# Last output projection: seven block products in place of eight for units 2 to 7

## What is computed

```python
y = jnp.concatenate([y_sb, y_lru], axis=-1)
h = h + jnp.einsum('bse,ed->bsd', y, w_out[l])
```

## Time and profile before

| | before |
|---|---|
| median of three runs | 2098.05 us (2097.89 to 2100.16) |
| profiled execution, span | 2098.9 us |
| PE, DVE, ACT, POOL busy | 99%, 68%, 47%, 9% of the span |
| unit 1 of the last projection ends, units 2 to 7 start | 1964.8 us |
| last matmul starts | 2095.29 us |

### The profile page before, as it was taken

One profiled execution on the slowest core, in us unless ns is written; L12 is line 12 of the kernel. 1 busy time (PEld: TensorE's weight loads), 2 busy tenths in 40 slices (PEclk: granted clock), 3 DMA queues, 4 the chain that ended last, 5 costly groups with the idle time before them and its releaser, 6 DMA issues. The chain is left out here.

```text
span 2098.9 us, 30066 instructions
## 1 busy us (share of the span) xinstructions
PE 2082.9 (99%) x9702; PEld 1734.5 (83%) x9702; DVE 1417.7 (68%) x2581; ACT 996.4 (47%) x1928; POOL 191.2 (9%) x197
## 2 busy tenths in 40 slices
PE   9999999999999999999999999999999999999999
PEld 7888888888888888888888788888888888888887
DVE  6677777777733568888888633677777677868432
ACT  6444444445422446666666633544454545446221
POOL 0111111112101000000000122200000000003000
PEclk9999999999999999999999999999999999999999
DMA  7324444445733624444444734533434334345742
GB/s 227 100 72 113 111 112 114 113 114 170 210 83 97 196 63 122 126 127 127 127 127 118 250 95 115 170 106 86 121 101 133 87 108 119 109 114 156 218 112 70
DMA packets 409917, 264.40 MB, mean 126 GB/s; under 512 B 20480, under 2 KB 382720, under 8 KB 409856
## 3 DMA queue, kind: packets, MB, share of 16 engines
q1 hardware_dynamic: 401120, 255.87, 43.1%
q10 hardware_dynamic: 8736, 7.74, 1.5%
HBM read 210.33 MB, written 24.12 MB: 112 GB/s over the span
## 5 line engine op out<-in xcount | busy, mean ns | idle before, releaser
L639 PE MATMUL pp<-act_hi,w_hi 128*128 128x512 f32 x2304 | 903.1, 392 | 6.9 <-DVE w_lo L613 4.2
L641 PE MATMUL pp<-act_hi,w_lo 128*128 128x512 f32 x2304 | 898.2, 390 | 0.0
L640 PE MATMUL pp<-act_lo,w_hi 128*128 128x512 f32 x2304 | 897.9, 390 | 0.0
L613 DVE TENSOR_TENSOR w_lo<-raw,w_hi 128x512 fp32r<-128x512 f32 x680 | 457.1, 704 | 360.7 <-ACT w_hi L605 359.8
L605 ACT ACTIVATE w_hi<-raw 128x512 fp32r<-128x512 f32 (+1 forms) x684 | 396.2, 622 | 456.2 <-PE pp L641 231.3
L639 PEld LDWEIGHTS pp<-act_hi,w_hi 128*128 128x128 f32 x2304 | 433.1, 188 | 100.9 <-DVE w_lo L613 6.0
L641 PEld LDWEIGHTS pp<-act_hi,w_lo 128*128 128x128 f32 x2304 | 432.9, 188 | 91.1
L640 PEld LDWEIGHTS pp<-act_lo,w_hi 128*128 128x128 f32 x2304 | 433.2, 188 | 87.3 <-issue 0.2
L658 POOL TENSOR_TENSOR pT_lo<-gathered,pT_hi 128x640 fp32r<-128x640 f32 x30 | 46.5, 1571 | 358.9 <-ACT pT_hi L654 358.9
L1318 ACT ACTIVATE prob<-ps,minus,q_scale 128x512 f32<-128x512 f32 (+1 forms) x64 | 39.0, 615 | 78.3 <-DVE minus L1398 78.3
L639 PE MATMUL ps<-act_hi,w_hi 128*128 128x512 f32 x176 | 69.3, 394 | 0.0
(11 more groups left out here) (435 smaller groups left out, 2755.1 us busy)
## 6 DMA issues: line engine op xcount, KB each, us to landing
raw<-w_in SPq DMA_DIRECT2D x48, 1024.0 KB, 5.9
raw<-swa_w_in SPq DMA_DIRECT2D x36, 1024.0 KB, 5.8
raw<-mla_w_in SPq DMA_DIRECT2D x23, 1024.0 KB, 5.7
raw<-mla_w_out SPq DMA_DIRECT2D x16, 1024.0 KB, 6.5
raw<-swa_w_out SPq DMA_DIRECT2D x16, 1024.0 KB, 6.1
raw<-w_out SPq DMA_DIRECT2D x16, 1024.0 KB, 6.9
gathered<-turned SPq DMA_DIRECT2D x224, 56.0 KB, 2.0
x_feature_major<-xT SPq DMA_DIRECT2D x8, 1024.0 KB, 9.7
```

The costliest lines, as they stand in the source:

```text
L613: q.eng.tensor_tensor(dst, raw_piece(tile, p), high, ALU.subtract).then_inc(s_lo, tile.ups(p))
L639: q.eng.matmul(psum[:, :], wh, ah, start=start and n == 0, stop=False)
L640: q.eng.matmul(psum[:, :], wh, al, start=False, stop=False)
L641: last = q.eng.matmul(psum[:, :], wl, ah, start=False, stop=stop and n == PIECE // P - 1)
```

## The change

Units 2 to 7 no longer take 16 chunks by 512 tokens in one sum. Each unit is a 2 by 2 block product: two output tiles (rows), two halves of the 16 chunks (inner), two halves of the tokens (`early`, `late`, 256 each). Seven products of 8 chunks by 256 tokens replace the eight: `11`, `12`, `22` on plain blocks, `s1`, `s2`, `s3` on sums of y blocks, and `s4` with a sum of weight blocks; `s1` to `s4` all use sums of weight blocks. A product is 24 matmuls of 128 by 256, in a PSUM bank of its own. Units 0 and 1 are made as before.

- `y_sums_G`: five steps on GpSimd, behind its last `act_lo`, make the y sums: (1) `chain` = late minus early of chunks 0 to 7; (2) chunk 15 put together again; (3) `chain` = late of chunks 8 to 15 minus `chain`; (4) late of 8 to 15 minus late of 0 to 7; (5) early of 8 to 15 minus `chain`. Steps 1, 3, 4 and 5 have 2048 elements in each partition. Chunks 8 to 14 are loaded again from HBM into `xT`, 1.75 MB, by a transfer that SP starts behind L844 and L845. `y_sums_A` and `y_sums_V` make the high and low halves of the four sums, 2048 elements each.
- Weights come as four blocks of 1024 columns for each unit, each with its own semaphore. `weight_sums` makes four sums of blocks on DVE, `split_hi` and `split_lo` the halves of the seven factors, in a ring of four places.
- ACT copies product `11`; DVE makes three partial sums and four final sums of 256 columns, and scales the old x; GpSimd adds partial sums to the old x, four times 256 columns for each unit.
- In the first unit of this kind DVE's order is: the four low halves of the y sums, weight sums `s1` and `s3`, old x twice, the low halves of `11` and `12`, then what is left of unit 1, then the low half of `s1` and so on.
- The two stores of a unit count on a semaphore each, and unit 1 puts its result into `acc` and `root`, since `d_y` is still read.

```diff
--- before.py
+++ after.py
+PLAIN_LAST = 2
+HALF_K, HALF_S = KC // 2, S // 2
+PRODUCTS = ("11", "12", "s1", "s2", "s3", "s4", "22")
+RING = (2, 3, 0, 1)
...
+        chain = low[:, 0:HALF_K * HALF_S].rearrange("p (c n) -> p c n", c=HALF_K)
+        w_sum = low[:, 8 * HALF_S:12 * HALF_S]
+        p1_sum, q_sum, u_sum = (low[:, (12 + n) * HALF_S:(13 + n) * HALF_S] for n in range(3))
...
+            q.eng.dma_start(xT[:, HALF_K:KC - 1, :], y_dram[HALF_K:KC - 1].rearrange("c p s -> p c s")).then_inc(s_ycopy, 16)
+            q.eng.wait_ge(s_lo, Tile("out3", PLAIN_LAST - 1, 1).count(PIECES - 1))
+            for b in ("11", "12", "22", "21"):
+                block(PLAIN_LAST, b)
+            store_out(q, 0, 0)
+            store_out(q, 0, 1)
+            q.eng.wait_ge(s_tlo, 4)
+            q.eng.dma_start(xT[:, HALF_K:KC, :], old_x(HALF_K, KC)).then_inc(s_xload[1], 16)
+            store_out(q, 1, 0)
+            store_out(q, 1, 1)
+            for i in range(PLAIN_LAST, units):
+                n = i - PLAIN_LAST
+                if i + 1 < units:
+                    q.eng.wait_ge(s_wsum, 4 * n + 3)
+                    q.eng.wait_ge(s_wlo, split_of(i, "11"))
+                    block(i + 1, "11")
+                    q.eng.wait_ge(s_wlo, split_of(i, "s3"))
+                    block(i + 1, "21")
+                    q.eng.wait_ge(s_wlo, split_of(i, "s4"))
+                    block(i + 1, "12")
+                    q.eng.wait_ge(s_wlo, split_of(i, "22"))
+                    block(i + 1, "22")
+                store_out(q, i, 0)
+                store_out(q, i, 1)
...
+        def strassen_T(q):
+            for i in range(PLAIN_LAST, KC // 2):
+                n, first = i - PLAIN_LAST, i == PLAIN_LAST
+                for product in PRODUCTS:
+                    q.eng.wait_ge(s_wlo, split_of(i, product))
+                    if product == "11":
+                        if first:
+                            q.eng.wait_ge(*q.at("V.x0", 0))
+                        else:
+                            q.eng.wait_ge(s_part, n)
+                    if first and product == "12":
+                        q.eng.wait_ge(*q.at("V.x1", 0))
+                    if product in ("12", "s4", "22") and not first:
+                        q.eng.wait_ge(s_new, 4 * (n - 1) + {"12": 1, "s4": 3, "22": 4}[product])
+                    if product in ("s2", "s1", "s3") and not first:
+                        q.eng.wait_ge(s_sums, 3 * (n - 1) + 1 + ("s2", "s1", "s3").index(product))
+                    if first and product == "22":
+                        q.eng.wait_ge(*q.at("V.x0", 1))
+                    if first and product in ("s1", "s2", "s3", "22"):
+                        q.eng.wait_ge(s_tlo, 1 + ("s1", "s2", "s3", "22").index(product))
+                    high, low_ = ring_of(i, product, w_hi), ring_of(i, product, w_lo)
+                    for c in range(HALF_K):
+                        cols = slice(c * P, (c + 1) * P)
+                        m = products(q, product_bank(product), (high[:, cols], low_[:, cols]), y_of(product, c),
+                                     c == 0, c == HALF_K - 1)
+                    m.then_inc(s_product, 1)
...
+        def y_sums_A(q):
+            places = y_sum_places()
+            late = slice(HALF_S, S)
+            q.eng.wait_ge(*q.at("V.y", phase="stick", body=H3))
+            for n, (dst, src) in enumerate(((t1[:, 0], chain), (t2[:, 0], chain), (t3[:, 0], places[1]),
+                                            (act_hi[:, 0:HALF_K, late], places[0]))):
+                q.eng.wait_ge(s_tsum, (1, 3, 3, 4)[n])
+                if n == 3:
+                    q.eng.wait_ge(s_used, Tile("out3", PLAIN_LAST - 1, 1).used(1))
+                q.eng.activation(dst, src, ACT.Copy).then_inc(s_thi, 1)
+        def y_sums_V(q):
+            places = y_sum_places()
+            late = slice(HALF_S, S)
+            for n, (dst, src, high) in enumerate(((t1[:, 1], chain, t1[:, 0]), (t2[:, 1], chain, t2[:, 0]),
+                                                  (t3[:, 1], places[1], t3[:, 0]),
+                                                  (act_lo[:, 0:HALF_K, late], places[0], act_hi[:, 0:HALF_K, late]))):
+                q.eng.wait_ge(s_thi, n + 1)
+                q.eng.tensor_tensor(dst, src, high.bitcast(F32), ALU.subtract).then_inc(s_tlo, 1)
+        def y_sums_G(q):
+            early, late = slice(0, HALF_S), slice(HALF_S, S)
+            before, after = y_sum_places()
+            last = HALF_K - 1
+            q.eng.wait_ge(*q.at("V.turned_lo", phase="stick", body=H3 - 1))
+            q.eng.wait_ge(*q.at("V.y_lru", phase="stick", body=H3 - 1))
+            q.eng.wait_ge(s_yload[0], 16 * LAYERS)
+            q.eng.tensor_tensor(chain[:, 0:last, :], y_lru[:, :, late], y_lru[:, :, early], ALU.subtract)
+            q.eng.tensor_tensor(chain[:, last, :], d_y[:, 1, late], d_y[:, 1, early], ALU.subtract).then_inc(s_tsum, 1)
+            q.eng.wait_ge(s_ylo_v, y_lo_count(KC - 1))
+            again = xT[:, KC - 1, :]
+            q.eng.tensor_tensor(again, act_hi[:, KC - 1, :].bitcast(F32), act_lo[:, KC - 1, :].bitcast(F32), ALU.add).then_inc(s_ycopy, 1)
+            q.eng.wait_ge(s_ycopy, 17)
+            q.eng.wait_ge(s_tlo, 1)
+            q.eng.tensor_tensor(chain, after, chain, ALU.subtract).then_inc(s_tsum, 1)
+            q.eng.wait_ge(s_tsum, 2)
+            q.eng.tensor_tensor(after[:, 0:last, :], after[:, 0:last, :], y_lru[:, :, late], ALU.subtract)
+            q.eng.tensor_tensor(after[:, last, :], after[:, last, :], d_y[:, 1, late], ALU.subtract).then_inc(s_tsum, 1)
+            q.eng.tensor_tensor(before, before, chain, ALU.subtract).then_inc(s_tsum, 1)
+        def split_hi(q, i, product):
+            g = split_of(i, product) - 1
+            if g < len(RING):
+                q.eng.wait_ge(s_used, Tile("out3", PLAIN_LAST - 1, 1).used(g))
+            else:
+                q.eng.wait_ge(s_product, g - len(RING) + 1)
+            n = i - PLAIN_LAST
...
+        def weight_sums(q, i, *wanted):
+            n = i - PLAIN_LAST
+            for s in wanted:
+                if s == "s1":
+                    q.eng.wait_ge(s_block["21"], 16 * (n + 1))
+                    q.eng.wait_ge(s_block["22"], 16 * (n + 1))
+                    if n:
+                        q.eng.wait_ge(s_wlo, split_of(i - 1, "s2"))
+                    m = q.eng.tensor_tensor(w_sum, raw_block("21"), raw_block("22"), ALU.add)
+                if s == "s3":
+                    q.eng.wait_ge(s_block["11"], 16 * (n + 1))
+                    q.eng.wait_ge(s_wsum, 4 * n + 1)
+                    m = q.eng.tensor_tensor(raw_block("21"), raw_block("11"), raw_block("21"), ALU.subtract)
+                if s == "s2":
+                    q.eng.wait_ge(s_wlo, split_of(i, "s1"))
+                    m = q.eng.tensor_tensor(w_sum, w_sum, raw_block("11"), ALU.subtract)
+                if s == "s4":
+                    q.eng.wait_ge(s_wlo, split_of(i, "12"))
+                    q.eng.wait_ge(s_wsum, 4 * n + 3)
+                    m = q.eng.tensor_tensor(raw_block("12"), raw_block("12"), w_sum, ALU.subtract)
+                m.then_inc(s_wsum, 1)
+        def split_lo(q, i, product):
+            q.eng.wait_ge(s_whi, split_of(i, product))
+            q.eng.tensor_tensor(ring_of(i, product, w_lo), weights_of(product), ring_of(i, product, w_hi).bitcast(F32),
+                                ALU.subtract).then_inc(s_wlo, 1)
+        def strassen_A(q):
+            for product in PRODUCTS[0:4]:
+                split_hi(q, PLAIN_LAST, product)
+            for i in range(PLAIN_LAST, KC // 2):
+                n = i - PLAIN_LAST
+                q.eng.wait_ge(s_product, split_of(i, "11"))
+                if n:
+                    q.eng.wait_ge(s_oldsum, 4 * (n - 1) + 1)
+                    q.eng.wait_ge(s_sums, 3 * (n - 1) + 1)
+                q.eng.activation(p1_sum, product_bank("11"), ACT.Copy).then_inc(s_part, 1)
+                for product in PRODUCTS[4:]:
+                    split_hi(q, i, product)
+                if i + 1 < KC // 2:
+                    for product in PRODUCTS[0:4]:
+                        split_hi(q, i + 1, product)
...
+            for i in range(PLAIN_LAST, KC // 2):
+                n, more = i - PLAIN_LAST, i + 1 < KC // 2
+                split_lo(q, i, "s3")
+                new(i, "12", 0, early, 1)
+                split_lo(q, i, "s4")
+                split_lo(q, i, "22")
+                q.eng.wait_ge(s_product, split_of(i, "s2"))
+                q.eng.wait_ge(s_part, n + 1)
+                if n:
+                    q.eng.wait_ge(s_oldsum, 4 * n)
+                q.eng.tensor_tensor(q_sum, product_bank("s2"), p1_sum, ALU.add).then_inc(s_sums, 1)
+                q.eng.wait_ge(s_sums, 3 * n + 1)
+                q.eng.tensor_tensor(u_sum, product_bank("s1"), q_sum, ALU.add).then_inc(s_sums, 1)
+                if more:
+                    scale_old(i + 1)
```

(62 more changed lines are left out.)

93 lines of the change are left out of this document (75 added, 18 removed).

## The result

The changed kernel takes 2114.78 us (median of 4 runs, 2112.44 to 2116.61); the kernel before, in the same comparison, 2099.11 (2097.89 to 2101.56). The ratio is 1.007, interval 1.0056 to 1.0084: slower by 0.7%, as forecast, and 6.9 us over the 2107.9 of the forecast. The profiled execution took 2113.65 us, of which the span is 2111.8. Above I took the span of the kernel before, 2098.9 us, for the time of its profiled execution, and that was probably 1.8 us too low. The forecast doesn't change by it: it is the median plus 9.8 us.

A forecast was written before the change was run, and what follows sets the result against it. PE alone was taken to bound units 2 to 7. The terms 2.0 + 16.0 + 2.2 - 10.0 - 0.4 = +9.8 us gave a median of 2107.9 us, with a range of 2101 to 2116.

The forecast's parts named there:

- What bounds the kernel, and the saving: Units 2 to 7: bound by PE alone; 1008 matmuls of 256 columns replace 576 of 512, saving 10.0 us.
- the 13 ns: Units 2 to 7: a matmul costs some 13 ns beside its columns, at 256 as at 512 columns.
- PE is fed in units 2 to 7: Units 2 to 7: DVE needs 17.9 to 19.9 us of PE's 20.1 in a unit; 0 taken for waits.
- Rival 3: Units 2 to 7: DVE becomes the bound, a unit takes 22 us, the kernel 2119; chance 0.06.
- The stall: Between unit 1 and first product `11`: PE waits 16.0 us behind the y sums, bounds 13.5 to 19.5.
- The last head: Last head, ahead of unit 1's end: GpSimd's step 1 slows its DVE chain, +2.0 us, bounds 0.5 to 3.0.
- The factor of 1.72: Last head: its DVE chain took 8.8 us under GpSimd's work against 5.13 with GpSimd idle.
- The low clock: Behind the stall: PE restarts at the low clock, a loss of 2.2 us, bounds 1.4 and 3.1.
- The tail: End of the kernel: a last addition of 256 columns and an earlier last matmul end give -0.4 us.
- all high bounds: Whole kernel: 2098.05 + 3.0 + 19.5 + 3.1 - 10.4 = 2113.3 us.
- Rival 1: Start of unit 2: the y sums are there in time, so faster; 2089.7 us with no stall; chance 0.09.
- rival 2: Start of unit 2: the terms cancel with a stall of 4 to 8 us, time about 2098; chance 0.08.

The follow-up runs named there:

- the halves experiment: The kernel before, with each matmul of units 2 to 7 made as two of 256 columns, same sums, no Strassen: 2107.91 us, 1.0037.
- the fastest kernel: Changed kernel with GpSimd's step 1 late, steps 3 to 5 on DVE, y copy ahead of old x, DVE and SP reordered: 2097.70 us, 0.9989.

## Why the prediction was right in its sign and low in its size

- **What bounds the kernel, and the saving: right.** The 0.1197 us of the earlier trace rows held in units 2 to 7 (1007 distances at 0.12), and the halves experiment shows the 13 ns by itself.
- **PE is fed in units 2 to 7: right.** I had 17.9 to 19.9 us of DVE work in 20.1; the trace has 18.0 to 18.7 in windows of 20. Rival 3 did not come, but it was near: one operation of 2048 elements more begins to bring it on.
- **The stall: right mechanism, mis-sized, 16.0 against 18.05.** The wait is where it was put, released by `split_lo` behind the four low halves. Step 3 starts 7.35 us before the end of unit 1 (1960.61 to 1967.96) where I had 9.2 (1955.6 to 1964.8): 1.9 of the 2.0 us. The part of the term that was mis-sized is the landing of y. The last head held SP's issue back as well (old x at 1946.15), as it did unit 1, so that cancels. The two transfers took 14.5 us from there, where 8.2 + 4.7 = 12.9 were forecast; another 0.2 is my slip, since 1951.1 + 4.7 is 1955.8 and not 1955.6. The likely cause of the 1.6 us is that transfers on the queue overlap: the first weight blocks are issued at 1955.22, while y is under way. From 1945.7 to 1960.6 the core moved 313 GB/s, 4.7 MB, of which old x (both transfers, 2048 KB) and y (1792 KB) are 3.9. The other 0.7 MB can only be weight blocks, and at that rate they are 2.3 us, an estimate. No run took them away. With y ahead of old x (the fastest kernel) the two again took 14.5 us, but y was there 9.3 us after its own issue, before DVE was ready for it.
- **The last head: right place, mis-sized, 2.0 against 3.9, outside its bounds of 0.5 to 3.0.** The factor of 1.72 was a mean over many short GpSimd instructions; one of 4.63 us holds a DVE operation to its end. About 1.5 us of the 3.9 is clock, which I had not looked for here: behind the wait of 3.63 us the matmuls from 1935.09 to 1938.4 run 0.43 apart, 7 or 8 of them at 0.2 more each.
- **The low clock: right, 2.2 against 2.0.** Matmuls of 256 columns are 0.21 apart until 1989.6. **The tail: right**, 0.4.
- **No luck in the sign.** The two misses, 1.9 and 2.05 us, go the same way, and nothing of note cancels them. The ledger's 13.7 over the 2098.05 that I started from would be 2111.8, under the 2113.3 that all high bounds gave together. The measured median of 2114.78 is 1.5 over those 2113.3, by what the medians have beyond the ledger, and still in the stated range up to 2116.
- **Rivals 1 and 2** needed a stall of 8 us or less. The late step 1 and the steps on DVE leave 11.1 us; only with another order on DVE, ACT and SP as well does it fall to 5.0, and there the kernel is as fast as rival 2 said, near 2098. Rival 1's 2089.7 was not reached by any kernel.
- My remark that `11` is late only since it stands behind the y sums on DVE was true of the order, and of no use by itself: with GpSimd's steps beside them, the low halves moved ahead are held as well (7.78 us for two).

## What to carry to other kernels

A block scheme that saves matmuls has to be paid where it starts: ask what PE does while the first operands are summed, and price each queue (DVE, GpSimd, SP) from there to the second unit, not only the steady state. Price GpSimd beside DVE by the length of one GpSimd instruction, not by a mean slowdown; here short instructions, or the same steps on DVE, cost less. In SP's order, what the next unit needs goes ahead of anything that waits for a late result. Of the 10 us that the fewer matmuls save, the best order found here keeps 2 to 3.
